# AdaLN modulation sums in a two-block transformer kernel: the operands of the summing matmuls exchanged, with a row copy and a transpose behind them

## What is computed

```python
sc = jax.nn.silu(c)
scc = jax.nn.silu(c_ctx)
...
m = (sc @ ada_w[i] + ada_b[i]).reshape(-1, N_MOD, D_MODEL)[:, :, None, :]
mc = (scc @ ada_w[i] + ada_b[i]).reshape(N_MOD, D_MODEL)[:, None, None, :]
x = x + 0.5 * m[:, 2] * swiglu(modulate(x, norm_g[i, 0], m[:, 0], m[:, 1]),
                               ffn_w_gate[i, 0], ffn_w_up[i, 0], ffn_w_down[i, 0])
```

## Time and profile before

| | |
|---|---|
| median of 3 runs | 2203.77 us (2202.48 to 2207.8) |
| the profiled execution | 2203.0 us, its span 2201.3 us |
| TensorE matmul busy | 2084.1 us, 95% |
| VectorE busy | 1439.4 us, 65% |
| ScalarE busy | 966.0 us, 44% |
| GpSimd busy | 215.9 us, 10% |
| chain that ended last | TensorE 81%, VectorE 12%, ScalarE 3%, issue 3% |

### The profile page before, as it was taken

One profiled execution on the slowest core, in us unless ns is written; L12 is line 12 of the kernel. 1 busy time (PEld: TensorE's weight loads), 2 busy tenths in 40 slices (PEclk: granted clock), 3 DMA queues, 4 the chain that ended last, 5 costly groups with the idle time before them and its releaser, 6 DMA issues.

```text
span 2201.3 us, 38485 instructions
## 1 busy us (share of the span) xinstructions
PE 2084.1 (95%) x16303; PEld 1982.2 (90%) x16303; DVE 1439.4 (65%) x1740; ACT 966.0 (44%) x1093; POOL 215.9 (10%) x193
## 2 busy tenths in 40 slices
PE   5899999999988999999999899999999988999996
PEld 4899999987756999999999899999999878999976
DVE  3546687779778966777744654466765555776553
ACT  2433443343333644334434443345444635634541
POOL 1000000010022101001000000002310000330000
PEclk9999999999999999999999899999999998999998
DMA  9677868853232437888555345545433423543410
GB/s 327 237 274 271 275 211 291 297 165 97 88 99 82 170 113 247 293 290 283 192 191 190 121 163 184 187 154 173 136 115 107 143 69 104 178 131 116 134 58 20
DMA packets 270793, 383.85 MB, mean 174 GB/s; under 512 B 8441, under 2 KB 230727, under 8 KB 270679
## 3 DMA queue, kind: packets, MB, share of 16 engines
q1 hardware_dynamic: 246983, 293.59, 41.0%
q0 software_dynamic: 22288, 85.02, 11.0%
q10 hardware_dynamic: 1408, 3.59, 0.4%
HBM read 381.06 MB, written 1.11 MB: 174 GB/s over the span
## 4 chain that ended last, share of the span: by engine, by line
PE 81%; DVE 12%; ACT 3%; issue 3%; DMA 0%; SPq 0%; DVEq 0%; ACTq 0%
PE bank L690 22%; PE bank L691 21%; PE bank L692 21%; PE bank L1143 3%; DVE w_hl L1859 1%; ACT w_hl L1405 1%; PE bank L720 1%; DVE conv_acc L2187 1%; PE bank L755 1%; PE bank L740 1%; PE bank L767 1%; DVE e_long L2238 1%; DVE ada_acc L1932 1%; DVE scratch L1893 1%; PE bank L769 1%
## 5 line engine op out<-in xcount | busy, mean ns | idle before, releaser
L1859 DVE TENSOR_TENSOR w_hl<-raw,w_hl 128x2048 fp32r<-128x2048 f32 (+1 forms) x281 | 642.5, 2287 | 396.1 <-ACT w_hl L1405 396.0
L1405 ACT ACTIVATE w_hl<-raw 128x2048 fp32r<-128x2048 f32 (+1 forms) x281 | 532.3, 1894 | 218.1 <-PE bank L692 214.7
L690 PE MATMUL bank<-u_hl,w_hl 128*128 128x256 f32 x2080 | 590.9, 284 | 0.0
L691 PE MATMUL bank<-u_hl,w_hl 128*128 128x256 f32 x2080 | 586.3, 282 | 0.0
L692 PE MATMUL bank<-u_hl,w_hl 128*128 128x256 f32 x2080 | 586.0, 282 | 0.0
L690 PEld LDWEIGHTS bank<-u_hl,w_hl 128*128 128x128 f32 x2080 | 394.2, 190 | 8.5 <-issue 3.4
L691 PEld LDWEIGHTS bank<-u_hl,w_hl 128*128 128x128 f32 x2080 | 394.1, 189 | 0.0
L692 PEld LDWEIGHTS bank<-u_hl,w_hl 128*128 128x128 f32 x2080 | 393.9, 189 | 0.0
L690 PE MATMUL bank<-h_hi,w_hl 128*128 128x256 f32 x800 | 226.8, 283 | 4.0 <-DVE h_lo L1956 4.0
L691 PE MATMUL bank<-h_lo,w_hl 128*128 128x256 f32 x800 | 225.9, 282 | 0.0
L692 PE MATMUL bank<-h_hi,w_hl 128*128 128x256 f32 x800 | 225.8, 282 | 0.0
(11 more groups left out here) (405 smaller groups left out, 4059.7 us busy)
## 6 DMA issues: line engine op xcount, KB each, us to landing
ada<-in_ada_w POOLq DMA_DIRECT2D x72, 1024.0 KB, 7.0
raw<-in_w_in SPq DMA_DIRECT2D x60, 1024.0 KB, 5.2
raw<-in_ffn_w_gate SPq DMA_DIRECT2D x55, 1024.0 KB, 7.3
raw<-in_ffn_w_up SPq DMA_DIRECT2D x55, 1024.0 KB, 5.3
raw<-in_ffn_w_down SPq DMA_DIRECT2D x55, 1024.0 KB, 5.2
raw<-in_ssd_w_in SPq DMA_DIRECT2D x20, 1024.0 KB, 5.3
raw<-in_w_out SPq DMA_DIRECT2D x16, 1024.0 KB, 5.2
raw<-in_ssd_w_out SPq DMA_DIRECT2D x8, 1024.0 KB, 5.3
```

Of the source, the lines that this page charges most:

```text
L690: pe.matmul(out_, wh, xh, start=start, stop=False, skip_group_check=True)
L691: pe.matmul(out_, wh, xl, start=False, stop=False, skip_group_check=True)
L1405: nc.scalar.activation(whi[slot][:, 0:n], raw[slot][:, 0:n], ACT.Copy).then_inc(S["hi_done"], 1)
L1859: ve.tensor_tensor(wlo[slot][:, 0:n], raw[slot][:, 0:n], whi[slot][:, 0:n].bitcast(F32), ALU.subtract)\
```

## The change

The sum over partitions in the "one" pairs gets its operands exchanged. 32 columns of `ones` are the weights of a column strip, and a 128-column block of `ada_acc` moves; the four blocks go to the four strips of bank 2 (`ada_sum_one`). The sums lie in rows then. ScalarE copies the bank's first 128 columns into `ada_rows[0]` (`rows_keep`), TensorE transposes them into bank 3 with the same `ada_turn` as the "both" pairs, and VectorE adds the bias from every 32nd column. A new semaphore, `ada_summed`, goes from TensorE to ScalarE.

The sum stays where it was. The transpose stands behind the up projection in the loop, and in the last pair in the middle of the last down projection (`between`). The copy stands at the end of a pair in ScalarE's queue, and in the last pair between the rounding of the product and the roundings of the next stage's chunks. ScalarE's loop is split in two where the pairs change form.

```diff
-            def ada_turn_one(pair):
+            def ada_sum_one(pair):
 
                 pe.wait_ge(S["ada_done"], pair + 1)
                 for blk in range(4):
-                    m = pe.matmul(bank[3][:, blk:blk + 1], ada_acc[:, blk * P:(blk + 1) * P], ones[:, 0:1],
+                    m = pe.matmul(bank[2][32 * blk:32 * blk + 32, 0:P], ones[:, 0:32], ada_acc[:, blk * P:(blk + 1) * P],
                                   start=True, stop=True)
-                m.then_inc(S["ada_turned"], 1)
+                m.then_inc(S["ada_summed"], 1)
...
                     for b in range(KB):
+                        if b == KB // 2 and between:
+                            between()
...
-                    def turn_one():
+                    def sum_one():
+                        ada_sum_one(m0 - 1 + j)
+
+                    pe.wait_ge(S["mult_done"], pairs + j)
+                    hidden(g + 4, 1, None, j - 1, sum_one if ada_too == "one" else None)
+                    if ada_too == "one":
                         pe.wait_ge(S["mods_done"], 2 * (m0 - 1) + 2 * j)
-                        ada_turn_one(m0 - 1 + j)
-
-                    pe.wait_ge(S["mult_done"], pairs + j)
-                    hidden(g + 4, 1, None, j - 1, turn_one if ada_too == "one" else None)
+                        ada_turn(m0 - 1 + j, 3, 0, 0)
...
                     if ada_too == "one":
+                        ada_sum_one(m0 - 1 + j)
+
+                    def turn_last():
                         pe.wait_ge(S["mods_done"], 2 * (m0 - 1) + 2 * j)
-                        ada_turn_one(m0 - 1 + j)
+                        ada_turn(m0 - 1 + j, 3, 0, 0)
+
                     pe.wait_ge(S["h_done"], pairs + FP)
-                    down(g + 3 * FP - 1, False, True, 0, h2_hi, h2_lo)
+                    down(g + 3 * FP - 1, False, True, 0, h2_hi, h2_lo, turn_last if ada_too == "one" else None)
...
+                m0 = ADA_FIRST // 2 + (ADA_FFN // 2) * i
+
+                def rows_keep(pair):
+                    act.wait_ge(S["ada_summed"], pair - BOTH_PAIRS + 1)
+                    nc.scalar.activation(ada_rows[0][:, :], bank[2][:, 0:P], ACT.Copy).then_inc(S["ada_rows"], 1)
+
+                for j0, j1, ada_too in ADA_LOOPS[i]:
+                    with act.Fori(j0, min(j1, FP - 1)) as j:
+                        h_rounded(j)
+                        hi_r(g + 3 * j + 1, 1, j, 0)
+                        silu(j, g + 3 * j - 1)
+                        hi_r(g + 3 * j + 2, 2, j, 0)
+                        hi_r(g + 3 * j + 3, 3, j, 0)
+                        if ada_too == "one":
+                            rows_keep(m0 - 1 + j)
...
                 h_rounded(FP, h2_hi)
+                if ADA_LOOPS[i][-1][2] == "one":
+                    rows_keep(m0 - 2 + FP)
                 hi_at(g + 3 * FP)
                 hi_at(g + 3 * FP + 1)
...
-                ve.tensor_tensor(mods_all[:, bass.ds(4 * pair, 4), 0], bank[3][:, 0:4], cols[:, bass.ds(4 * pair, 4)],
+                ve.tensor_tensor(mods_all[:, bass.ds(4 * pair, 4), 0],
+                                 bank[3][:, 0:P].rearrange("p (b v) -> p b v", v=32)[:, :, 0], cols[:, bass.ds(4 * pair, 4)],
                                  ALU.add).then_inc(S["mods_done"], 2)
```

More of the change, by code:

```diff
@@ L363, in two_block_kernel @@
         make("hi_done", "chunk_used",
-             "ada_half", "ada_done", "ada_rows", "ada_acc", "ada_turned", "mods_done", "silu_c",
+             "ada_half", "ada_done", "ada_rows", "ada_acc", "ada_summed", "ada_turned", "mods_done", "silu_c",
              "cols_turned", "cols_done", "x_turned", "x_done",
@@ L820, in hidden, with down @@
                     m.then_inc(S["chunk_used"], 1)
-                def down(c, opens, closes, j=0, hh=h_hi, hl=h_lo):
+                def down(c, opens, closes, j=0, hh=h_hi, hl=h_lo, between=None):
                     take(c, j)
```

## The result

The changed kernel takes 2218.4 us, median of 4 runs (2216.99 to 2220.63), against 2203.9 of the kernel before (2202.48 to 2207.8). The ratio is 1.0070, with an interval of 1.0056 to 1.0084: slower, by more than the 0.3% that can be told from no change, and 4 us above the upper end of my range. The profiled execution took 2217.0 us, its span is 2215.3 us, 14.0 more than before. One of the six runs of a later version, the one that moves ScalarE's copy alone, took 5107 us; nothing here explains it, and it is left out of that version's comparison.

What follows compares the result with a forecast made beforehand. TensorE was taken to bound the loops, VectorE's chain the tails. Loop saving -4.6, tails +7.3, clock +2.6 and norms +0.4 gave +5.7 on 2203.8: 2209.5 us, range 2201 to 2214.

Steps and rivals of the forecast that it cites:

- Sum and transpose on TensorE: Per pair, the sum falls from 0.89 to 0.58 us and the transpose adds 0.11, saving 0.20 us.
- Rival 3: Sum on TensorE: strips cost their share of the long run, 0.26 us; 7.4 us more saved, 2202 us; chance 0.07.
- 0.04 us remain: just hidden: Loop pairs: VectorE's product comes 0.45 us later, but a 0.04 us margin still keeps it from delaying TensorE.
- -4.4 over the intervals between sums: Loops and last loop sums to tails' sums: forecast -3.8 and -0.6 us, part of the 4.6 us saving.
- Rival 2: Loop pairs: VectorE's late addition becomes the bound, giving back 3.7 us at 0.65 us delay; +9.4, 2213 us; chance 0.22.
- The tail: Ends of FFN0, FFN1, FFN2: x done 2.8, 1.75 and 2.8 us later, together 7.3 us more, uncovered.
- The clock: Behind longer TensorE waits: clock falls behind FFN0, 2.6 us more; norms behind FFN1 and FFN2 add 0.4 for both.
- The unedited rest: Stretches no edit touches: no change forecast, apart from -0.2 us for the loop sum without its own interval.
- slowed norms: Behind FFN1 and FFN2: norms slowed by 1 us each, said to end near rival 2's time.

Runs made afterwards that it cites:

- second pair of profiles: The kernel before and the changed kernel, each run once more unchanged: 2202.7 us (ratio 1.0003) and 2218.4 us (1.0077).
- filled norms: Unread extra matmuls in three norms and behind last down projections: 2196.5 us added to the version with both moves, 2201.4 us added to the kernel before.
- the version with both moves: Changed kernel with the loops' transpose 12 matmuls earlier, and tail copy and addition behind the last rounding: 2203.8 us (1.0008), repeated 2205.2 us (1.0016).

## Why the prediction was wrong

- **Sum and transpose on TensorE: right.** 0.55 us against 0.58 forecast, the transpose 0.11, so 0.22 us a pair where nothing waits. The edges of the earlier trace rows were the thing to use. Rival 3, which charged no edges and took 0.26 us from the same rows, had half of what the trace shows. The Trainium skill's span of a pack (TensorE: Matmul & The Clock Gate, Part 3: Packing small matmuls), one tile's duration and about 4 ns for each further one, has no such edges either.
- **"0.04 us remain: just hidden": this step failed.** I had the product 0.45 us late, it is 0.95 late. The addition costs 0.16 and not 0.1, and behind it the loop's end costs 0.39 to 0.44, which I had not looked for: the instructions are in VectorE's queue, but no row of before shows them, since there they lay under a wait. Pairs take 17.97 us in FFN1 and 18.10 in FFN2, against 17.71 where nothing waits, 0.26 and 0.39 more; by my margin it would have been 0.46, so slightly more was spare than I wrote. In place of -4.4 over the intervals between sums it became +0.6 (+1.3 in the loops, -0.7 in the last ones): 5.0 us of the miss. Moving the addition over the loop's end, or the transpose ahead, brings the 17.7 us back. Rival 2 had this mechanism, at 0.22, and its sign, pairs that get slower, was named. A margin of 0.04 us, beside a delay that was itself unsure by some tenths, deserved more than that chance.
- **The tail: right in size, and in mechanism but for one half.** +2.63, +1.54 and +2.61 against 2.8, 1.75 and 2.8. Moving the two instructions takes 6.0 of the 6.8 us back. I had VectorE's wait for the transpose in FFN1 alone. It stands in FFN0 and FFN2 too, hidden behind the late rounding: with ScalarE's copy moved, 1.5 us of the 2.6 remain. ScalarE's wait was 2.00 us (forecast "about 2"), TensorE's 4.16 (forecast 4.2).
- **The clock: right in kind, mis-sized.** It does fall behind FFN0, and costs 1.4 instead of 2.6 us: by the windows it was full for the first 0.8 us and back about 4.2 us behind the start, and I had it low from the start to 5.7 us behind. Behind the norms I took 0.4 us for both, and it was 1.0 and 2.4. My reason was that the clock falls there already. Falling earlier it takes the whole of L720 with it (4.42 us instead of 2.44), and all that follows up to the first projection matmuls. Together +4.8 instead of +3.0; in the second pair of profiles +3.8.
- **The unedited rest: put at nothing (-0.2 for the sum without an interval), +1.8 in this pair of profiles and +4.3 in the second.** The two profiles of before agree there to 0.1 us, and all nine of the changed kernel and its versions without filled norms lie 1.8 to 8.1 us above them. So a part of the miss seems to come with the change, outside the places that it edits. Its cause stays open.
- **The range.** I treated "VectorE becomes the bound" (2213) and "slowed norms" as two ways to the same time. They are separate places and both came: 2209.5 + 5.0 + 1.8 - 0.5 is 2215.8; 2.0 more lie in the rest (1.8, and the 0.2 forecast there as a gain), and 0.6 between profiles and medians. The upper end should have been the sum of the costs and not the dearest single one.

## What to carry to other kernels

When an edit makes an instruction near a loop's end wait that never waited, count what stands between it and the next one in the queue: register and branch instructions cost nothing under a wait, and 0.4 us behind one. An instruction that waits for another engine belongs behind those in its queue whose results somebody is short of: here ScalarE's copy behind the roundings, and VectorE's addition behind the subtraction. A saving of 5 us in the edited stretches of this kernel did not reach the total, since stretches that nobody edited grew: add up the untouched part too, over more than one profile and many runs. The mean granted clock hints at it, but puts no price on it.

## What was not expected of the hardware

- A loop's register operation and branch on VectorE, exposed behind a wait: 0.44 us from the addition to the product, 0.05 without them.
- Behind a wait of 0.73 us in front of FFN2's norm the clock fell in the middle of L720's 20 one-column matmuls (2.79 instead of 2.44 us); behind a wait of 3.42 us all of them ran at a granted clock of 0.50, that is 1.2 GHz (4.42 us).
- Unedited code differs by several microseconds between profiles of kernels, and of one kernel: the mixer stretch takes 389.3 and 393.0 us in two profiles of before, the part behind the last sum takes 1111.2 and 1109.1 for before, 1111.3 and 1116.5 for after. Two executions of before with the same span had mean clocks of 0.958 and 0.954. The Trainium skill (TensorE: Matmul & The Clock Gate, Part 1: The HAM clock gate) says that the number of slow matmuls at a kernel's start differs between runs of the same kernel; here the spread shows in the middle of one too.
- Extra matmuls that nobody reads took 8.7 us off the median of the version with both moves, and 1.0, which is within the measurement, off that of the kernel before.
